# Context loaded behind the modulation pairs, and its norm done beside the first weight blocks

## What is computed

```python
sh1, sc1, ... = ada(c, ada_w[i], ada_b[i])             # silu(c) @ w + b
csh1, csc1, ... = ada(c_ctx, ada_w[i], ada_b[i])
h_l = rmsnorm(x, norm1_g[i]) * (1 + sc1) + sh1         # x: 256 x 1024
h_c = rmsnorm(ctx, norm1_g[i]) * (1 + csc1) + csh1     # ctx: 256 x 1024
p_lat = h_l @ w_in                                     # 1024 x 2208
p_ctx = h_c @ w_in                                     # of it only keys, values (288 columns)
cq, ckv, k_pe = p[..., :384], p[..., 384:640], p[..., 640:672]
b_gate, c_gate, u = split(p[..., 672:], 3)             # 512 columns each
q = rmsnorm(cq, q_norm_g) @ w_uq;  kv = rmsnorm(ckv, kv_norm_g) @ w_ukv
z = c_gate * u;  y = b_gate * conv(z)
```

## Time and profile before

| what | value |
|---|---|
| median of 3 runs | 1772.34 us (1771.25 to 1774.88) |
| the profiled execution's own time | 1772.96 us |
| its span, first to last instruction | 1771.2 us |
| PE busy | 1642.6 us (93%) |
| DVE / ACT / POOL busy | 751.2 (42%) / 438.8 (25%) / 124.9 us (7%) |
| DMA | 586.36 MB, mean 331 GB/s |
| chain that ended last | PE 77%, DMA 9%, SP's queue 7%, DVE 5% |

### The profile page before, as it was taken

How to read it: one execution, slowest core, us unless ns; L and a number is a source line. 1 busy time by engine, 2 the same in 40 slices (tenths; PEclk the granted TensorE clock), 3 DMA queues, 4 the chain that set the end, 5 groups by cost and what they waited for, 6 DMA issues and landing times.

```text
span 1771.2 us, 22164 instructions
## 1 busy us (share of the span) xinstructions
PE 1642.6 (93%) x8392; PEld 987.4 (56%) x8392; DVE 751.2 (42%) x1182; ACT 438.8 (25%) x692; POOL 124.9 (7%) x151
## 2 busy tenths in 40 slices
PE   5999899999999999999999999999959898799776
PEld 2964678888878888776334443344414352345222
DVE  5576588777388786543222212122202220122022
ACT  3535554543445443442100000000000000000001
POOL 1942010000500000010000000000000000000000
PEclk9999999999999999999999999999979998999888
DMA  9624468884468877429999999999999999999994
GB/s 386 232 93 167 157 246 329 295 326 159 182 255 308 322 273 273 184 90 372 412 420 420 421 420 420 421 420 420 421 421 421 420 421 421 420 421 420 421 421 189
DMA packets 103503, 586.36 MB, mean 331 GB/s; under 512 B 12368, under 2 KB 13648, under 8 KB 50800
## 3 DMA queue, kind: packets, MB, share of 16 engines
q1 hardware_dynamic: 103408, 585.09, 83.4%
HBM read 584.00 MB, written 1.05 MB: 330 GB/s over the span
## 4 chain that ended last, share of the span: by engine, by line
PE 77%; DMA 9%; SPq 7%; DVE 5%; issue 2%; ACT 1%; DVEq 0%; ACTq 0%
PE psum L1296 22%; PE psum L1312 11%; SPq L440 5%; PE psum L939 4%; PE psum L941 4%; PE psum L940 4%; PE psum L1267 3%; DMA mraw<-gu_dram 3%; PE psum L1057 3%; PE psum L960 2%; PE psum L962 2%; PE psum L961 2%; PE psum L1325 2%; DMA araw<-ada_dram 2%; PE psum L1153 2%
## 5 line engine op out<-in xcount | busy, mean ns | idle before, releaser
L1296 PE MATMUL psum<-mraw,xsat 128*64 128x512 f32 (+2 forms) x1544 | 424.6, 636 | 38.0 <-DMA mraw<-gu_dram 24.3
L1296 PEld LDWEIGHTS psum<-mraw,xsat 128*64 128x64 f32 (+2 forms) x1544 | 140.2, 144 | 259.5 <-issue 258.1
L1312 PE MATMUL psum<-mraw,xsat 128*64 128x512 f32 (+2 forms) x680 | 177.3, 624 | 13.7 <-DMA mraw<-dn_dram 6.3
L1296 PE MATMUL psum<-mlast,xsat 128*64 128x512 f32 (+2 forms) x408 | 151.6, 673 | 16.7 <-DMA mraw<-gu_dram 16.7
L939 PE MATMUL psum<-wh,ah 128*128 128x512 f32 x352 | 139.4, 396 | 3.5 <-DVE al L1991 2.6
L1877 POOL TENSOR_TENSOR wl<-raw,wh 128x256 fp32r<-128x256 f32 x132 | 113.8, 897 | 367.2 <-DVE work L2018 216.9
L941 PE MATMUL psum<-wh,al 128*128 128x512 f32 x352 | 137.3, 390 | 0.0
L940 PE MATMUL psum<-wl,ah 128*128 128x512 f32 x352 | 137.2, 390 | 0.0
L2532 DVE TENSOR_TENSOR oacc<-psum,oacc 128x512 f32<-128x512 f32 x60 | 38.7, 686 | 216.0 <-PE psum L1325 216.0
L2039 DVE TENSOR_TENSOR wl<-raw,wh 128x1024 fp32r<-128x1024 f32 x88 | 104.8, 1232 | 32.9 <-ACT wh L1581 32.9
L1843 ACT ACTIVATE xsat<-psum 128x512 f32<-128x512 f32 x16 | 9.6, 597 | 433.0 <-PE psum L1345 433.0
(11 more groups left out here) (389 smaller groups left out, 2512.0 us busy)
## 6 DMA issues: line engine op xcount, KB each, us to landing
mraw<-gu_dram SPq DMA_DIRECT2D x193, 1024.0 KB, 22.1
mraw<-dn_dram SPq DMA_DIRECT2D x85, 1024.0 KB, 24.4
araw<-ada_dram SPq DMA_DIRECT2D x128, 512.0 KB, 4.7
mlast<-gu_dram SPq DMA_DIRECT2D x51, 1024.0 KB, 20.7
raw<-ffa_dram SPq DMA_DIRECT2D x44, 1024.0 KB, 5.3
mlast<-dn_dram SPq DMA_DIRECT2D x34, 1024.0 KB, 24.3
raw<-ffb_dram SPq DMA_DIRECT2D x44, 512.0 KB, 5.2
raw<-blk_dram SPq DMA_DIRECT2D x34, 512.0 KB, 4.7
```

What stands on the lines that cost most here:

```text
L1296: last = mm(ps[4 + n][a * w:(a + 1) * w, :], xs[:, k * P + a * w:k * P + (a + 1) * w], slot_columns(slot, i * 2 * D + n * 512), start=Fals ...
L1312: last = mm(ps[n][a * w:(a + 1) * w, :], at[:, k * P + a * w:k * P + (a + 1) * w], slot_columns(slot, i * D + n * 512), start=(k == 0), st ...
```

## The change

The context's load moves behind the eight pairs and blocks 0 and 1. Its squares, sum, root and scaling move from the head to places beside blocks 0 to 6. Block 0 is multiplied by h as loaded, in float32, without a split (8 products instead of 24). The gate b's blocks come first, then the queries. Products of constants stand between the pairs. The chunks of the next modulation move from behind blocks 4 to 11 to behind blocks 7 to 14. ACT's table for the root is loaded in the head by a dummy instruction. ACT's context halves (`ctx_hi`) are one instruction a tile instead of two. The semaphore counts follow.

```diff
-B_Q, B_CB, B_KV, B_KPE, B_CC, B_CU = 0, 3, 7, 9, 10, 14
+B_CB, B_Q, B_KV, B_KPE, B_CC, B_CU = 0, 4, 7, 9, 10, 14
...
             def blk(b):
+                if b == NFIRST_RAW:
+                    sp.wait_ge(s_blk, 1)
                 if b >= NFIRST_RAW:
...
-            sp.dma_start(xc[:, :], xc_d).then_inc(s_xin, 16)
             ada_pair(1)
             sp.dma_start(con[:, :], con_d).then_inc(s_con, 16)
             for k in range(2, 8):
                 ada_pair(k)
-            for b in range(NRAW):
+            for b in range(2):
                 blk(b)
+            sp.wait_ge(s_sum, 1)
+            sp.dma_start(xc[:, :], xc_d).then_inc(s_xin, 16)
+            blk(2)
...
-            mm(ps[3][:, :], ones, work[:, 0, :], start=True, stop=True).then_inc(s_sum, 1)
+            mm(ps[3][:, 0:T], ones, work[:, 0, 0:T], start=True, stop=True).then_inc(s_sum, 1)
             for k in range(2, 6):
                 ada_rows(k)
+                keep_clock(3)
             row_columns(0)
-            for k in range(6, 8):
-                ada_rows(k)
+            ada_rows(6)
+            keep_clock(3)
+            ada_rows(7)
+            keep_clock(2)
             row_columns(1)
 
-            keep_clock(5)
+            keep_clock(2)
+            pe.wait_ge(s_raw[0], RAW_LOADED[0])
+            for j in range(DJ):
+                pe.wait_ge(s_h, j + 1)
+                last = mm(ps[0][:, 0:T], raw[:, j * P:(j + 1) * P], work[:, j, 0:T], start=(j == 0), stop=(j == DJ - 1))
+            last.then_inc(s_blk, 1)
...
-            for b in range(B_O):
-                block_product(b, 2 * T if B_KV <= b <= B_KPE else T, fresh={0: (s_hl, 0), B_KV: (s_hlx, 0)}.get(b))
+            for b in range(1, B_O):
+                block_product(b, 2 * T if B_KV <= b <= B_KPE else T, fresh={1: (s_hl, 0), B_KV: (s_hlx, 0)}.get(b))
+                if b == 3:
+                    pe.wait_ge(s_ntx, 1)
+                    mm(ps[3][:, T:2 * T], ones, work[:, 0, T:2 * T], start=True, stop=True).then_inc(s_cqsum, 1)
...
             link(A(csil[:, :], vec[:, 0:16], ACT.Sigmoid))
-            act.wait_ge(s_xin, 32)
+            A(warm[:, :], V("eps", 0, 1), ACT.Sqrt).then_inc(s_hi, 1)
+            act.wait_ge(s_xin, 16)
             for j in range(DJ):
-                A(work[:, j, 0:T], x[:, j, :], ACT.Square)
-                A(work[:, j, T:2 * T], xc[:, j * TC:(j + 1) * TC], ACT.Square).then_inc(s_sq, 1)
-            norm_root(0, 2 * T)
+                norm_square(0, j)
+            norm_root(0)
...
-            for b in range(3):
-                block_hi(b)
+            block_hi(1)
             h_hi(0)
+            block_hi(2)
+            act.wait_ge(s_xin, 32)
+            for j in range(DJ):
+                A(work[:, j, T:2 * T], xc[:, j * TC:(j + 1) * TC], ACT.Square).then_inc(s_cqs, 1)
 
             def ctx_hi(j):
-                act.wait_ge(s_ntx, j + 1)
-                link(A(work[:, j, T:2 * T], work[:, j, T:2 * T], ACT.Identity, bias=modx[:, j:j + 1], scale=gsx[:, j:j + 1]))
-                A(ah3[:, j, T:2 * T], work[:, j, T:2 * T], ACT.Copy).then_inc(s_hhx, 1)
-
-            for b in range(3, 7):
-                block_hi(b)
-                ctx_hi(2 * (b - 3))
-                ctx_hi(2 * (b - 3) + 1)
-            block_hi(7)
-            for j in range(3):
-                act.wait_ge(s_ev, j + 1)
-                A(sqf[:, j * T:(j + 1) * T], cq[:, j, :], ACT.Square).then_inc(s_cqs, 1)
-            for b in range(8, 11):
+                act.wait_ge(s_ntx, j + 2)
+                A(ah3[:, j, T:2 * T], work[:, j, T:2 * T], ACT.Identity, bias=modx[:, j:j + 1]).then_inc(s_hhx, 1)
+
+            for b in range(3, 6):
                 block_hi(b)
             act.wait_ge(s_cqsum, 1)
+            A(rt[:, T:2 * T], ps[3][:, T:2 * T], ACT.Sqrt, bias=V("eps"), scale=1.0 / D).then_inc(s_cqrt, 1)
+            block_hi(6)
+            for j in range(4):
+                ctx_hi(j)
+            block_hi(7)
+            for j in range(4, DJ):
+                ctx_hi(j)
+            block_hi(8)
+            for j in range(3):
+                act.wait_ge(s_ev, B_Q + j + 1)
+                A(sqf[:, j * T:(j + 1) * T], cq[:, j, :], ACT.Square).then_inc(s_cqs, 1)
+            for b in range(9, 11):
+                block_hi(b)
...
+            def first_norm():
+                dve.wait_ge(s_rt, 1)
+                link(V_.reciprocal(rstd[:, 0:T], rt[:, 0:T]))
+                for j in range(DJ):
+                    TTn(work[:, j, 0:T], x[:, j, :], rstd[:, 0:T], ALU.mult).then_inc(s_nt, 1)
+                first_mods()
+                norm_gain(_V["n1"], 0)
+                for j in range(DJ):
+                    dve.wait_ge(s_nt, j + 1)
+                    TS(work[:, j, 0:T], work[:, j, 0:T], gs[:, j:j + 1], m_col(0, j), ALU.mult, ALU.add).then_inc(s_h, 1)
+                for j in range(DJ):
+                    dve.wait_ge(s_hh, j + 1)
+                    TTn(al3[:, j, 0:T], work[:, j, 0:T], f32(ah3[:, j, 0:T]), ALU.subtract).then_inc(s_hl, 1)
...
+            def ctx_sum(part):
+                for j in part:
+                    dve.wait_ge(s_cqs, j + 1)
+                    ins = TTn(work[:, 0, T:2 * T], work[:, 0, T:2 * T], work[:, j, T:2 * T], ALU.add)
...
+            def ctx_scaled(part):
+                for j in part:
+                    STT(work[:, j, T:2 * T], xc[:, j * TC:(j + 1) * TC], gsx[:, j:j + 1], rstd[:, T:2 * T], ALU.mult, ALU.mult
+                        ).then_inc(s_ntx, 1)
...
-                if b < 4:
-                    ctx_lo(2 * b)
-                    ctx_lo(2 * b + 1)
-                elif b < 12:
-                    ada(ADA_FIRST + b - 4)
+                if b in (0, 1, 2):
+                    ctx_sum(((1, 2), (3, 4), (5, 6, 7))[b])
+                elif b == 3:
+                    dve.wait_ge(s_cqrt, 1)
+                    link(V_.reciprocal(rstd[:, T:2 * T], rt[:, T:2 * T]))
+                    ctx_scaled(range(4))
+                elif b == 4:
+                    ctx_scaled(range(4, DJ))
+                    ctx_lo(0)
+                    ctx_lo(1)
+                elif b in (5, 6):
+                    for k in range(3):
+                        ctx_lo(3 * b - 13 + k)
+                elif b < 15:
+                    ada(ADA_FIRST + b - 7)
```

64 lines of the change are left out of this document (31 added, 33 removed).

## The result

The changed kernel takes **1780.51 us** (median of 6 runs, 1778.48 to 1783.02) where the kernel before, timed beside it, takes 1771.69 us (6 runs, 1768.02 to 1774.88). The ratio is 1.0049, with a 95% interval of 1.0037 to 1.0061: slower by 8.8 us, outside the predicted range and on the side that had a chance of 0.11. The profiled execution took 1783.02 us, its span 1781.1 us (before 1771.2). It is the slowest of the six, 2.5 us above their median, so what its trace shows may be more than the typical run loses. One of twelve executions of a later kernel ("ACT's roundings first, POOL waits once") was in a slow state of the chip, 2447 us at a mean granted clock of 0.63, and is not in that kernel's ratio.

A forecast was written before the change was run, and what follows sets the result against it. PE, busy from 46 to 105 us, was the bound, POOL the hidden second, DMA pacing the head. Gaining 3.0 us at block 7, losing 3.3 behind it, plus 0.3 for clock: +0.6 on 1772.34 gives 1772.9 us, range 1769.2 to 1775.6.

The forecast's parts named there:

- the side that had a chance of 0.11: Whole kernel: slower by over 0.2%, from half clock, POOL held off, or both late block loads.
- Head: Before block 0: pairs land 2.56 us sooner without the context in front; modulation sums at 32.6 us, where it was 35.7.
- Block 0: First block, multiplied unsplit: eight products end at 37.8 us; DVE's copy comes 7.6 us sooner than before.
- Blocks 1 to 6: POOL's 24 pieces beside about 24 DVE instructions take 21.2 us; block 7 starts at 59.3, a gain of 3.0 us.
- Blocks 7 to 17: Late chunks hold block 15's load in SP's queue; block 17 ends at 105.7 us, 0.3 us later than before.
- B: Rival: half clock through block 0, its products ending at 42.9 us; block 17 4.0 us later, 1776.3 us; chance 0.05.
- C: Rival, blocks 1 to 6: DVE holds POOL off for whole instructions; block 7 at 65.6, total 1779 us; chance 0.04.
- the sum of 27.5 us: Blocks 1 to 6: upper bound for POOL's 24 pieces, each 0.725 us plus a whole DVE instruction of 0.42 us.
- A: Rival, blocks 7 to 17: block 15 is ready in time, the 3.0 us gain reaches the end; 1769.3 us; chance 0.17.
- No later stage can add to it: Behind the first 105 us: their gain or loss reaches the kernel's end whole, with nothing added later.

The follow-up runs named there:

- ACT's roundings first, POOL waits once: Kernel with ACT's block roundings ahead of its context work, plus POOL waiting ahead of block 12 until DVE has used chunk 17; 1771.81 us, ratio 0.9985 to 1.0008.
- the last one: Kernel with ACT's roundings first and POOL waiting once, with the changed kernel's keepers between the pairs put back; 1771.73 us, ratio 0.9998.

## Why the prediction was wrong, step by step

The forecast was 1772.9 us and the measured median is 1780.51. By the traces block 17 was to be copied at 105.7 and was copied at 113.83, 8.1 us late. This adds up from three places: block 7 was copied 3.3 us late (64.7 forecast, 3.0 ahead of before's 67.72; measured 68.04), PE began block 16 another 2.1 us late (34.5 us behind that copy forecast, 36.6 measured), and blocks 16 and 17 took 9.2 us instead of 6.5.

**Head: right in kind, 2 us short.** I had the sums at 32.6; they came at 34.56. The pairs land as summed (in the kernel without keepers PE starts the sixth as it lands, at 22.95; 22.85 forecast), but a pair takes 0.99 us of PE with what follows it and three keepers 1.50, where I had 0.9 and 1.3, and PE works through that from pair to pair.

**Block 0: the mis-sized term.** Predicted copy 37.9, measured 41.95. The products ended near 39.85, where I had 37.8: these 2 us are the head's. (The sum also has a slip. Two tiles at 0.72 us and six at 0.35 from 33.65 on end at 37.2, not 36.7; the eight took 3.45 us. The first came 0.44 us behind the sums and not 1.05, which hid it.) The other 2 us are DVE, which takes its eight differences and the context's gain before it looks at block 0 (38.37 to 41.76 above). The sum had this work as POOL's burden and nowhere as DVE's own queue ahead of the copy.

**Blocks 1 to 6: a wait that the sum did not have.** I priced 24 pieces with 24 DVE instructions at 21.2 us. They took 16.86 + 3.56 = 20.4 us: the price was right. What was not in the sum is that ACT's list is in order. It puts block 2 behind the eight tiles of h (I had that, at 38.1; it came at 39.85) and blocks 6 and 7 behind the context's root and scaled tiles (I did not have that; 1.85 us of POOL). Predicted start of block 7 59.3, measured 62.26: 1.8 us late from the head, 1.85 us for ACT's list, 0.8 us less for the pieces. The kernels with ACT's list reordered bear this out: block 7 starts at 60.38 in the last one, behind a block 0 that was no sooner.

**Blocks 7 to 17: the largest error.** The mechanism was the right one, and I had its beginning: chunk use late, load behind it in the queue. POOL idled before blocks 13, 14 and 15 and PE stood ahead of blocks 15 and 16, as foretold. I expected a loss of 3.3 us behind block 7 and got 8.1 (45.8 us from copy to copy instead of 37.7). Up to the use of chunk 19, begun 6.8 us behind the copy of block 9 (I had 6.4), the chain is nearly as summed; it began 3.3 us later, as the copy of block 7 did. The failing term is the start of block 16: I had POOL's split of block 15 as what it waits for and took its load for done. That load hangs on chunk 20 in the same queue, was issued 1.9 us behind block 15's, and took 8.35 us where I had 4.9 for such a load. One load alone does not tell how long the second of two in a row takes. While it was under way the 16 DMA engines were full (a share of 1.0) and moved 3.0 MB at 357 GB/s, more than the 2.1 MB of the at most four loads then under way, so the loads issued behind it, at 94.03, 94.45 and 94.93, took their part too (an estimate from these rates). How long it takes varies: issued 1.9 us behind block 15's it took 6.9 us in the kernel before with late chunks and 6.6 us with keepers ahead of block 16, and there, and without keepers, block 16 did wait for POOL as forecast, 34.9 to 35.5 us behind the copy of block 7 (34.5 forecast). A third term was missing altogether. Behind the gap of 3.7 us that the late load opened, block 16 ran at half clock: 2.3 us by the two traces compared above.

**The rivals.** B, half clock through block 0, did not come: the granted clock was 1.00 in every stretch up to 103 us. It fell where nobody had put keepers. (A granted clock of 1.00 does not exclude slow products: the pairs at 6.96, 11.92 and 15.29 us took 1.93 to 1.94 us, that at 19.08 took 1.07.) C had the price of a POOL piece wrong in the stretch that it was about. The Trainium skill (SBUF — State Buffer, "Who interferes with whom") says that whichever engine starts first has the shared ports for its whole instruction and the other blocks fully. Where DVE was ahead, the rows agree: the piece at 39.93, started while DVE took its last differences back to back, took 1.81 us instead of 0.72, and the piece beside the chunk instruction at 100.31 took 1.71. Where POOL works piece after piece, a piece beside one of DVE's 256-column instructions takes 0.91, 0.19 more than a free one, and the sum of 27.5 us by the whole-instruction rule was wrong. The same section says that issue order and not the shape decides who blocks. The two kinds of case above fit that, but the 9.22 us instruction does not follow from it: it had started before eleven pieces that went ahead of it. A did not come either.

**"No later stage can add to it": true only on average.** From the copy of block 17 to the end it takes 1665.8 us in the profiled run of before and 1667.3 in that of the change; over all 16 profiled executions shown here 1661.8 to 1669.3, without relation to the edit. That spread of 7.5 us is as large as most differences looked for, so block 17 in the trace tells more than one span does.

**What stays open.** How often the long instruction comes in the runs that were not profiled, and what in the timing of the two engines starts it. Whether the load of block 16 takes 8.35 us and the clock falls in every run of the change, or mainly in the profiled one. Whether keepers would hold the clock through a gap of 3.7 us. Taking the context's norm off DVE was not tried, and the new order of the blocks was not tested by itself.
